# Scores of the next pair of heads, spread between the query tiles of the RWKV-7 stage

## The chip, the cores and the metric

The kernel runs on one core of one Trainium2 chip. The metric is the device time in microseconds of one execution of the whole program, as the median of the runs shown. Engines are named as the profile names them: PE is TensorE, DVE is VectorE, ACT is ScalarE, POOL is GpSimd, SP is SyncE, which issues most transfers.

## The reference, cut to what matters

The program is a two-layer diffusion backbone in float32 over 256 context and 256 latent tokens of width 1024. Layer 0 mixes tokens with a Hyena long convolution and a dense SwiGLU, layer 1 with bidirectional RWKV-7 and a top-2-of-8 expert SwiGLU. The change lies in RWKV-7, whose 16 heads of 64 channels follow this recurrence, forward and backward over context and latent tokens:

```
def step(S, inp):
    r_t, w_t, k_t, v_t, a_t, b_t = inp
    sa = jnp.einsum('bhvk,bhk->bhv', S, a_t)
    S = S * w_t[:, :, None, :] + sa[..., None] * b_t[:, :, None, :] + v_t[..., None] * k_t[:, :, None, :]
    return S, jnp.einsum('bhvk,bhk->bhv', S, r_t)
```

The kernel computes it in chunks of 64 tokens. Within a chunk it needs the products of all `a` with all `b` (called its own scores here), of `k` with `a` (key scores) and of `b` and `k` with the queries `r` (out scores), the inverse of a triangular matrix made from the own scores, and then one state per chunk boundary.

## The kernel before, in words

The heads are taken two at a time: eight pairs, `pair(i, more)`, each some 65 us long. Every engine has its own instruction stream, written out by hand, and each instruction waits on counting semaphores through `step(engine, group, name, pair)`: the names of a group stand in one ordered list (`_pair_steps`), and a wait is for a name's place in it. `settle` puts one wait-and-count instruction in the stream.

What a pair needs from the tokens themselves, called "ahead", is computed for the next pair while the present one runs: keys, rates, decays, values, queries and gate. TensorE's stream of a pair is, in order:

1. own scores S (line 1355, 32 products of 64x64 into banks 0 and 1; 64 matmul records, since each float32 product is two), key scores K (also line 1355, banks 2 and 3), out scores O (line 1375). S waits for VectorE's `a_1` of this pair and `g_ready_1` of the last, K for ScalarE's `out_copy`, O for ScalarE's `log_var`.
2. two turns of `At` (line 1223), which wait for ScalarE's copy of the gate out of bank 6.
3. the loop over four levels of the triangular inverse, 32x32 products: `level_first` (line 1299) waits for VectorE's transposed joins of S and, on entering the loop, for ScalarE's two score copies (line 2047), which themselves follow VectorE's joins of S (lines 2778 and 2781); then `level_second` (line 1310).
4. further turns, the last level, the keys of the next pair, products that build the chunk states (lines 1434 to 1504), and seven state steps (lines 1499 and 1504) with the tiles of the next pair's values (line 1273) between them. VectorE finishes `a_1` and `g_ready_1` before it makes the states of step 7.
5. the query tiles 0 to 3 of the next pair (line 1282, 128x256), the mean sum (line 1514), query tiles 4 to 7, the variance sum (line 1521), the gate products (lines 1289 and 1290). Then the next pair begins with S.

ScalarE at this place does, in order: `out_copy`, the square, the query copy (line 2027), Ln of the variance sum and Exp (lines 2095 and 2098, each with a table load), the gate copy (line 2031), the two score copies (line 2047). VectorE does `centred`, the multiplication of the queries with their decays, and then the joins of S, the masks of K and of O. SyncE loads the weights of the pair after next once the gate products are done (line 812). In the last pair the tiles of the output projection (line 1344, 128x256) stand between the state steps in place of the values.

Of the kernel before, what the change touches and what calls it, by code (L numbers as in the profile page):

```python
# [31 lines left out]
P = 128  # L32
D = 1024
KT = D // P
SEQ = 256
T = 2 * SEQ
NB = T // P
# [8 lines left out]
C = 64  # L46
# [123 lines left out]
def _pair_steps():  # L170


    pe = [f"{name}_{h}" for name in ("scored", "keys_scored", "out_scored") for h in range(2)]
    pe += ["a_turned_0", "a_turned_1", "b_turned_0", "b_turned_1", "k_turned_0", "k_turned_1", "v_turned"]
    pe += ["z_0", "z_1", "bonus_sum"]
    pe += [f"wu_{h}{d}" for h in range(2) for d in range(2)] + ["m_sum", "n_sum", "g_sum"]
    pe += [f"moved_{st}_{d}" for st in range(1, 7) for d in range(2)] + ["out_sum", "mean_sum", "var_sum"]

    act = ["score_copy_0", "score_copy_1", "a_copy_0", "a_copy_1", "b_copy_0", "b_copy_1", "k_copy_0", "k_copy_1"]
    act += ["v_copy", "spread_0", "spread_1", "z_copy_0", "z_copy_1"]  # L180
    act += [f"wu_copy_{h}{d}" for h in range(2) for d in range(2)]
    act += ["out_copy", "square", "log_var", "norm"]

    dve = []
    for h in range(2):
        dve += [f"joined_even_{h}", f"joined_0_{h}"]
    dve += ["keys_masked_0", "keys_masked_1", "out_masked_0", "out_masked_1", "chunk_decay"]
    dve += ["bonus", "inverse_0", "inverse_1", "n_ready_0", "n_ready_1", "state_1_0", "state_1_1"]
    dve += ["m_ready_0", "m_ready_1", "g_ready_0", "g_ready_1"]
    dve += [f"state_{st}_{d}" for st in range(2, 8) for d in range(2)]  # L190
    dve += ["centred"]
    finish = ["scaled", "shifted", "pair_out"]

    pool = ["g_start_0", "g_start_1", "gate_copy", "eye_0", "eye_1"]

    ahead_pe = ["keys", "rate_0", "rate_1", "decay_0", "decay_1", "key_sum", "values", "queries", "gate"]
    ahead_act = ["key_copy", "rate_sig_0", "rate_sig_1", "decay_sig_0", "decay_sig_1", "key_log", "key_norm"]
    ahead_act += ["e_incl_0", "e_inv_0", "e_excl_0", "e_incl_1", "e_inv_1", "e_excl_1"]
    ahead_act += ["value_copy", "query_copy", "gate"]
    ahead_dve = ["key_raw", "scan_0", "scan_1"]  # L200
    for d in range(2):
        ahead_dve += [f"rate_used_{d}", f"key_rated_{d}", f"bonus_key_{d}"]
    ahead_dve += ["key_unit"]
    for d in range(2):
        ahead_dve += [f"last_decay_{d}", f"k_{d}", f"b_{d}", f"a_{d}"]
    ahead_dve += ["r_0", "r_1", "bonus_query", "bonus_in"]
    ahead_pool = ["key_square", "b_raw_0", "b_raw_1", "next_digits"]
    return dict(pair_products=pe, pair_copies=act, pair_vectors=dve, pair_pool=pool, pair_finish=finish, ahead_products=ahead_pe,
                ahead_copies=ahead_act, ahead_vectors=ahead_dve, ahead_pool=ahead_pool)
# [44 lines left out]
def one(steps, name):  # L254


    names = STEPS[steps]
    assert names[PLACE[steps] % len(names)] == name, (steps, name, names[PLACE[steps] % len(names)])
    PLACE[steps] += 1
    return 1  # L260
# [74 lines left out]
def build(nc, a, out, consts):  # L335
    ctx = ExitStack()
    with ctx, nc.allow_non_contiguous_dma(reason="a few short columns"):
        sems = {}

        def sem(name):  # L340
            if name not in sems:
                sems[name] = ctx.enter_context(nc.semaphore(name))
            return sems[name]

        arena = ctx.enter_context(nc.sbuf_tensor("arena", [P, ARENA], F32))
        bank = [ctx.enter_context(nc.psum_tensor(f"bank{i}", [P, 512], F32)) for i in range(8)]
# [186 lines left out]
        last = mark()  # L533
# [122 lines left out]
        def hd(h):  # L656
            return slice(HN * h, HN * h + HN)

        def settle(eng):

            eng.sem_inc(sem("settled"), 1)
# [18 lines left out]
        def step(eng, steps, name, item):  # L680

            eng.wait_ge(sem(steps), (item + 1) * len(STEPS[steps]) + STEPS[steps].index(name) + 1)
# [188 lines left out]
        def _(pe):  # L871
# [405 lines left out]
            def ahead_queries(j, tiles):  # L1277
                if tiles[0] == 0:
                    pe.wait_ge(sem("ld_pair"), j * LD_PAIR + LD_QUERIES)
                    step(pe, "ahead_copies", "rate_sig_1", j)  # L1280
                for k in tiles:
                    last = mm(bank[7][:, 0:SEQ], wst[:, 0, k, :], XR[:, k, :], start=(k == 0), stop=(k == KT - 1))
                if tiles[-1] == KT - 1:
                    last.then_inc(sem("ahead_products"), one("ahead_products", "queries"))

            def ahead_gate(j):
                pe.wait_ge(sem("ld_pair"), j * LD_PAIR + LD_PAIR)
                step(pe, "ahead_copies", "value_copy", j)
                mm(bank[6][:, 0:SEQ], g2a, G1a, start=True, stop=False)
                mm(bank[6][:, 0:SEQ], g2b[0:32, :], G1b[0:32, :], start=False, stop=True)\  # L1290
                    .then_inc(sem("ahead_products"), one("ahead_products", "gate"))
# [46 lines left out]
            def out_products(first, last):  # L1338

                for t in range(first, last):  # L1340
                    k, m = t // KT, OUT_ORDER[t % KT]
                    if t % KT == 0:
                        pe.wait_ge(sem("ld_out"), 16 * (k + 1))
                    mm(out_sum(m), WO[k][:, m * P:(m + 1) * P], YT[:, k, :], start=(k == 0 and m % 2 == 0), stop=False,
                       skip_group_check=True)

            def pair(i, more):

                def scores(name, b0, left, right):
                    for x in range(2 * NB):  # L1350
                        d, b = divmod(x, NB)
                        for s_ in range(2):
                            t = slice(b * P + s_ * C, b * P + s_ * C + C)
                            for h in range(2):
                                last = mm(bank[b0 + h][hd(s_), x * C:x * C + C], left[d][hd(h), t], right[d][hd(h), t],
                                          start=True, stop=True)
                                if x == 2 * NB - 1 and s_ == 1:
                                    last.then_inc(sem("pair_products"), one("pair_products", f"{name}_{h}"))

                step(pe, "ahead_vectors", "a_1", i)  # L1360
                step(pe, "pair_vectors", "g_ready_1", i - 1)
                settle(pe)
                scores("scored", 0, At, Bt)
                step(pe, "pair_copies", "out_copy", i - 1)
                settle(pe)
                scores("keys_scored", 2, Kt, At)
                step(pe, "pair_copies", "log_var", i - 1)
                step(pe, "ahead_vectors", "r_1", i)
                settle(pe)
# [137 lines left out]
                last.then_inc(sem("pair_products"), one("pair_products", "out_sum"))  # L1507

                if more:
                    ahead_queries(i + 1, range(0, 4))  # L1510
                else:
                    out_products(16, 19)
                step(pe, "pair_copies", "out_copy", i)
                mm(bank[4][:, 0:SEQ], heads64, YF, start=True, stop=True)\
                    .then_inc(sem("pair_products"), one("pair_products", "mean_sum"))
                if more:
                    ahead_queries(i + 1, range(4, KT))
                else:
                    out_products(19, 23)
                step(pe, "pair_copies", "square", i)  # L1520
                mm(bank[5][:, 0:SEQ], heads64, YS, start=True, stop=True)\
                    .then_inc(sem("pair_products"), one("pair_products", "var_sum"))
                if more:
                    ahead_gate(i + 1)
                else:
                    out_products(23, OUT_TILES)

# [10 lines left out]
                ahead_values(0, [k])  # L1538
            pe.wait_ge(sem("xm_ready"), 6 * KT)
            ahead_queries(0, range(KT))  # L1540
            pe.wait_ge(sem("lora_taken"), 4)
            ahead_gate(0)
            for i in range(KT - 1):
                pair(i, True)
            pair(KT - 1, False)
# [791 lines left out]
        def _(dve):  # L2337
# [432 lines left out]
            def pair(i, more):  # L2770

                def first_join(h):
                    step(dve, "pair_products", f"scored_{h}", i)
                    step(dve, "pair_pool", f"eye_{h}", i - 1)
                    settle(dve)
                    scores = bank[h][:, :].rearrange("p (d b c) -> p d b c", d=2, c=C)
                    for j, name in enumerate(("joined_even", "joined_0")):
                        dve.copy_predicated(by_dir(TM[h], HC), each_block(first_bits[j]), scores[:, :, :, HC * j:HC * j + HC])\
                            .then_inc(sem("pair_vectors"), one("pair_vectors", f"{name}_{h}"))
                        step(dve, "pair_vectors", f"{name}_{h}", i)  # L2780
                    dve.transpose(TN[h].rearrange("p b c -> p (b c)"), TM[h].rearrange("p b c -> p (b c)"))\
                        .then_inc(sem("level_ready"), 1)
                    dve.sem_inc(sem("level_turned"), 1)
# [13 lines left out]
                for h in range(2):  # L2797
                    first_join(h)
                for h in range(2):
                    step(dve, "pair_products", f"keys_scored_{h}", i)  # L2800
                    dve.tensor_tensor(by_dir(AakT[h], C), by_dir(bank[2 + h][:, :], C), each_block(keys_mask), ALU.mult)\
                        .then_inc(sem("pair_vectors"), one("pair_vectors", f"keys_masked_{h}"))
                for h in range(2):
# [307 lines left out]
```

## Time and profile before

| | |
|---|---|
| median of 3 runs | 2436.03 us (2432.66 to 2442.88) |
| the profiled execution | 2433.53 us, its span 2431.7 us |
| mean granted TensorE clock | 0.982 |
| TensorE busy | 2327.2 us (96%) |
| VectorE, ScalarE busy | 1586.3 us (65%), 1265.7 us (52%) |
| chain that ended last | PE 91%, DVE 3%, issue 3%, ACT 1%, DMA 1% |
| the eight pairs of heads | some 840 to 1362 us of the span |

The chain that ended last is followed back from the last instruction; "issue" in it, and as a releaser of idle time, is time in which an engine waited for nothing that the profile shows. A matmul record overlaps its neighbours, so the distance from start to start tells what it takes in a stream, and its own duration does not.

### The profile page before, as it was taken

How to read it: one execution, taken by the hardware profiler on the slowest of the kernel's cores; microseconds unless marked ns; L12 is line 12 of the kernel's file. 1: busy time of each engine (PE TensorE's matmuls, PEld its weight loads, DVE VectorE, ACT ScalarE, POOL GpSimd, SP SyncE). 2: the span in 40 equal slices, each digit the busy share in tenths (PEclk: the TensorE clock that was granted, in tenths of full speed). 3: DMA queues.
4: the chain of work that ended last, by engine and by line, in shares of the span. 5: the costliest groups of instructions: out<-in, count | busy, mean ns of one | idle time of the engine just before them, and what ended most of it. 6: DMA issues, size and time to landing. Idle time of an engine off the chain costs nothing.

```text
span 2431.7 us, 57067 instructions
## 1 busy us (share of the span) xinstructions
PE 2327.2 (96%) x24762; PEld 1889.2 (78%) x24762; DVE 1586.3 (65%) x1810; ACT 1265.7 (52%) x1400; POOL 208.8 (9%) x196
## 2 busy tenths in 40 slices
PE   8999999999999888988988899999999999999998
PEld 5677576888887466767766688988888888888887
DVE  3544876222333945555555388888888888888887
ACT  4322025222222844444434277777777777777774
POOL 2000642000000221111111000000000000000000
PEclk9999999999999999999989999999999999999999
DMA  8465126333224201111112469999999999999993
GB/s 295 171 242 219 52 87 173 87 103 87 100 91 133 89 23 32 32 32 32 32 32 72 175 257 365 338 368 335 368 333 369 333 370 337 366 338 363 342 362 133
DMA packets 249079, 490.41 MB, mean 202 GB/s; under 512 B 14615, under 2 KB 107567, under 8 KB 248623
## 3 DMA queue, kind: packets, MB, share of 16 engines
q1 hardware_dynamic: 247214, 481.31, 55.8%
q10 hardware_dynamic: 1730, 7.10, 0.9%
q8 instruction: 109, 1.79, 0.3%
q14 instruction: 26, 0.21, 0.0%
HBM read 486.29 MB, written 2.10 MB: 201 GB/s over the span
## 4 chain that ended last, share of the span: by engine, by line
PE 91%; DVE 3%; issue 3%; ACT 1%; DMA 1%; SPq 0%; POOL 0%; DVEq 0%; ACTq 0%
PE bank L1626 26%; PE bank L1653 13%; PE bank L1159 3%; PE bank L1160 3%; PE bank L1161 3%; PE bank L1299 2%; PE bank L1273 2%; PE bank L1065 2%; PE bank L1036 2%; PE bank L1310 2%; PE bank L1037 2%; PE bank L1038 2%; PE bank L1177 2%; PE bank L1176 2%; PE bank L1178 2%
## 5 line engine op out<-in xcount | busy, mean ns | idle before, releaser
L2970 DVE TENSOR_TENSOR w_low<-expert_w,w_high 128x1792 fp32r<-128x1792 f32 (+2 forms) x384 | 769.1, 2024 | 125.3 <-ACT w_high L2169 123.6
L2169 ACT CAST w_high<-expert_w 128x1792 fp32r<-128x1792 f32 (+2 forms) x384 | 652.9, 1701 | 247.0 <-PE bank L1626 154.3
L1626 PE MATMUL bank<-w_high,xg_high 128*128 128x448 f32 x1024 | 294.5, 369 | 4.0 <-DVE xg_low L2960 4.0
L1626 PE MATMUL bank<-w_low,xg_high 128*128 128x448 f32 x1024 | 292.1, 367 | 0.0
L1626 PE MATMUL bank<-w_high,xg_low 128*128 128x448 f32 x1024 | 291.7, 366 | 0.0
L1626 PEld LDWEIGHTS bank<-w_high,xg_high 128*128 128x128 f32 x1024 | 191.5, 189 | 19.9 <-DVE xg_low L2960 4.2
L1626 PEld LDWEIGHTS bank<-w_low,xg_high 128*128 128x128 f32 x1024 | 193.4, 189 | 15.3
L1626 PEld LDWEIGHTS bank<-w_high,xg_low 128*128 128x128 f32 x1024 | 193.2, 189 | 15.2
L1653 PE MATMUL bank<-w_high,hid_high 128*128 128x512 f32 x448 | 175.4, 392 | 0.0
L1653 PE MATMUL bank<-w_high,hid_low 128*128 128x512 f32 x448 | 174.7, 390 | 0.0
L1653 PE MATMUL bank<-w_low,hid_high 128*128 128x512 f32 x448 | 174.5, 389 | 0.0
L1159 PE MATMUL bank<-u_high,ring_high 128*128 128x512 f32 x352 | 139.4, 396 | 2.1 <-DVE u_low L2615 2.0
L1160 PE MATMUL bank<-u_low,ring_high 128*128 128x512 f32 x352 | 139.1, 395 | 0.0
L1161 PE MATMUL bank<-u_high,ring_low 128*128 128x512 f32 x352 | 138.5, 393 | 0.0
L2634 DVE TENSOR_TENSOR arena<-arena,bank 128x512 f32 (+1 forms) x22 | 15.1, 688 | 127.5 <-ACT arena L1932 127.5
L1653 PEld LDWEIGHTS bank<-w_high,hid_low 128*128 128x128 f32 x448 | 84.1, 188 | 17.8
L1653 PEld LDWEIGHTS bank<-w_low,hid_high 128*128 128x128 f32 x448 | 84.2, 188 | 16.7
L1653 PEld LDWEIGHTS bank<-w_high,hid_high 128*128 128x128 f32 x448 | 84.2, 188 | 16.6
L1932 ACT ACTIVATE arena<-bank 128x512 f32<-128x512 f32 x22 | 13.2, 599 | 158.9 <-PE bank L1161 158.9
L2788 DVE COPY_PREDICATED arena<-arena,bank 128x256 f32<-128x256 int32 x64 | 28.4, 444 | 81.7 <-PE bank L1310 81.7
L1159 PEld LDWEIGHTS bank<-u_high,ring_high 128*128 128x128 f32 x352 | 66.6, 189 | 18.1 <-issue 2.9
L2037 ACT COPY arena<-bank 128x256 f32<-128x256 f32 x80 | 29.4, 382 | 97.5 <-PE bank L1299 97.4
(427 smaller groups left out, 4106.8 us busy)
## 6 DMA issues: line engine op xcount, KB each, us to landing
expert_w<-in_moe_w_dram SPq DMA_DIRECT2D x192, 1792.0 KB, 9.4
arena<-in_mod_w_dram SPq DMA_DIRECT2D x48, 1024.0 KB, 8.1
arena<-in_ffn_w_dram SPq DMA_DIRECT2D x44, 512.0 KB, 5.1
arena<-in_hy_w_in_dram SPq DMA_DIRECT2D x12, 1024.0 KB, 5.2
arena<-in_rw_w_rkv_dram SPq DMA_DIRECT2D x48, 256.0 KB, 2.7
arena<-in_ffn_w_dram SPq DMA_DIRECT2D x11, 1024.0 KB, 4.8
arena<-in_hy_w_out_dram SPq DMA_DIRECT2D x4, 1024.0 KB, 9.1
arena<-in_rw_w_out_dram SPq DMA_DIRECT2D x8, 512.0 KB, 3.5
```

Of the source, the lines that this page charges most:

```text
L1036: pe.matmul(bank[m % 4][:, :], wh[:, k, :], uh, start=(k == 0), stop=False)
L1037: pe.matmul(bank[m % 4][:, :], wh[:, k, :], ul, start=False, stop=False)
L1038: last = pe.matmul(bank[m % 4][:, :], wl[:, k, :], uh, start=False, stop=(k == KT - 1))
L1065: last = pe.matmul(bank[2 * part + f][:, :], fwd[:, tt, (2 * part + f) * P:(2 * part + f + 1) * P], ZT[:, 2 * s + tt, half * 512:half * 51 ...
L1159: pe.matmul(bank[b + h][:, :], wh[:, c, :], uh, start=(k == 0), stop=False)
L1160: pe.matmul(bank[b + h][:, :], wh[:, c, :], ul, start=False, stop=False)
L1161: last = pe.matmul(bank[b + h][:, :], wl[:, c, :], uh, start=False, stop=(k == KT - 1))
L1176: pe.matmul(bank[m][:, :], wh[:, o, :], hh, start=first, stop=False)
L1626: last = pe.matmul(bank[b0 + v][:, 0:EH], x[:, k, :], w_[:, kk, v * EH:v * EH + EH], start=(k == 0 and x is XGH and w_ is wh), stop=(k == ...
L1653: last = pe.matmul(bank[4 + half][:, :], x[:, f, :], w_[:, f - 4 * i_, :], start=(c == 0 and f == 0 and x is HTH and w_ is wh), stop=(c == ...
L2169: act.copy(high_piece(kind, n), piece(kind, ering[q % ERN], n // 2, n % 2))\
L2970: dve.tensor_tensor(piece(kind, low[s], n // 2, n % 2), piece(kind, ering[s], n // 2, n % 2), high_piece(kind, n).bitcast(F32), ALU.subtract)\
```

## The change

Line 1355's products leave `pair` and become two functions of a range of blocks. The own scores of the next pair are issued block by block, each block (4 products, 8 records) behind the query tile of the same number. The key scores of the next pair are issued in two halves, the first four blocks between the variance sum and the gate products, the other four behind the gate. Their semaphore names move from the group `pair_products` to `ahead_products`, and VectorE waits for them there. The waits that S and K had stand before their first blocks as before. In front of the first pair all own scores stand between queries and gate, and all key scores behind the gate. The number of products, waits and copies is the same.

```
-    pe = [f"{name}_{h}" for name in ("scored", "keys_scored", "out_scored") for h in range(2)]
+    pe = [f"{name}_{h}" for name in ("out_scored",) for h in range(2)]
...
+    ahead_pe = ["keys", "rate_0", "rate_1", "decay_0", "decay_1", "key_sum", "values", "queries", "scored_0", "scored_1",
+                "gate", "keys_scored_0", "keys_scored_1"]
...
+            def scores(i, name, b0, left, right, blocks):
+                if blocks[0] == 0:
+                    if name == "scored":
+                        step(pe, "ahead_vectors", "a_1", i)
+                        step(pe, "pair_vectors", "g_ready_1", i - 1)
+                    else:
+                        step(pe, "pair_copies", "out_copy", i - 1)
+                    settle(pe)
+                for x in blocks:
+                    d, b = divmod(x, NB)
+                    for s_ in range(2):
+                        t = slice(b * P + s_ * C, b * P + s_ * C + C)
+                        for h in range(2):
+                            last = mm(bank[b0 + h][hd(s_), x * C:x * C + C], left[d][hd(h), t], right[d][hd(h), t],
+                                      start=True, stop=True)
+                            if x == 2 * NB - 1 and s_ == 1:
+                                last.then_inc(sem("ahead_products"), one("ahead_products", f"{name}_{h}"))
...
                 if more:
-                    ahead_queries(i + 1, range(0, 4))
+                    for k in range(4):
+                        ahead_queries(i + 1, range(k, k + 1))
+                        own_scores(i + 1, range(k, k + 1))
...
                 if more:
-                    ahead_queries(i + 1, range(4, KT))
+                    for k in range(4, KT):
+                        ahead_queries(i + 1, range(k, k + 1))
+                        own_scores(i + 1, range(k, k + 1))
...
                 if more:
+                    key_scores(i + 1, range(4))
                     ahead_gate(i + 1)
+                    key_scores(i + 1, range(4, 2 * NB))
...
             ahead_queries(0, range(KT))
+            own_scores(0, range(2 * NB))
             pe.wait_ge(sem("lora_taken"), 4)
             ahead_gate(0)
+            key_scores(0, range(2 * NB))
```

## Rows read from the trace of the kernel before

**Rows 1.** The page, busy time and share of the span, instructions.

```profile
PE 2327.2 (96%) x24762; PEld 1889.2 (78%) x24762; DVE 1586.3 (65%) x1810; ACT 1265.7 (52%) x1400; POOL 208.8 (9%) x196
```

**Rows 2.** Waits of PE, 905 to 1316 us: line, releaser, us, times, longest.

```profile
PE bank L1310 <- issue: 17.2, 7, 3.0
PE bank L1299 <- issue: 5.6, 11, 1.5
```

**Rows 3.** DMA queues, 905 to 1316 us: packets, MB, share of 16 engines.

```profile
q8 instruction: 61, 1.00, 1.0%
```

**Rows 4.** Timeline of PE, pair 2 to 3: start us, us, instruction, count, idle before.

```profile
972.97 1.99 PE L1282 MATMUL bank<-arena 128*128 128x256 f32 x8
975.23 1.89 PE L1282 MATMUL bank<-arena 128*128 128x256 f32 x8
977.39 0.59 PE L1289 MATMUL bank<-arena 128*128 128x256 f32 x2
978.54 2.10 PE L1355 MATMUL bank<-arena 64*64 64x64 f32 x128
980.45 1.11 PE L1375 MATMUL bank<-arena 64*64 64x64 f32 x64
983.18 1.58 PE L1299 MATMUL bank<-arena 32*32 32x32 f32 x128 [0.60 <-DVE arena L2781]
984.65 0.39 PE L1310 MATMUL bank<-arena 32*32 32x32 f32 x22
...
987.48 0.75 PE L1310 MATMUL bank<-arena 32*32 32x32 f32 x49 [2.45 <-issue]
```

**Rows 5.** Timeline of ACT at the same place.

```profile
977.16 0.38 ACT L2027 COPY arena<-bank 128x256 f32<-128x256 f32 x1 [0.85 <-PE bank L1282]
977.55 1.28 ACT L2095 ACT_TABLE_LOAD   x1
...
980.96 0.35 ACT L2031 COPY arena<-bank 128x256 f32<-128x256 f32 x1
...
982.15 0.59 ACT L2047 COPY arena<-bank 128x512 f32<-128x512 f32 x1 [0.35 <-DVE arena L2778]
```

**Rows 6.** Timeline of PE, state steps of the last pair.

```profile
1353.21 0.33 PE L1499 MATMUL bank<-arena 64*64 64x64 f32 x4
...
1353.82 1.13 PE L1344 MATMUL bank<-arena 128*128 128x256 f32 x4
1354.88 0.33 PE L1499 MATMUL bank<-arena 64*64 64x64 f32 x4
```

**Rows 7.** Timeline of PE, pair 3 to 4.

```profile
1045.20 0.45 PE L1375 MATMUL bank<-arena 64*64 64x64 f32 x13 [1.71 <-issue]
1045.58 1.09 PE L1223 MATMUL bank<-arena 128*128 128x128 f32 x8
...
1049.36 0.39 PE L1299 MATMUL bank<-arena 32*32 32x32 f32 x24 [1.46 <-issue]
1049.57 1.25 PE L1310 MATMUL bank<-arena 32*32 32x32 f32 x103
1053.77 0.43 PE L1310 MATMUL bank<-arena 32*32 32x32 f32 x16 [2.95 <-issue]
```

**Rows 8.** Timeline of PE, first level of pairs 2, 5, 6, 7 and 8.

```profile
919.80 0.92 PE L1310 MATMUL bank<-arena 32*32 32x32 f32 x68
923.09 1.07 PE L1310 MATMUL bank<-arena 32*32 32x32 f32 x60 [2.37 <-issue]
...
1114.28 0.97 PE L1299 MATMUL bank<-arena 32*32 32x32 f32 x70 [0.98 <-issue]
...
1118.14 1.09 PE L1310 MATMUL bank<-arena 32*32 32x32 f32 x62 [2.37 <-issue]
...
1181.02 1.16 PE L1310 MATMUL bank<-arena 32*32 32x32 f32 x108 [2.11 <-issue]
...
1247.82 0.74 PE L1310 MATMUL bank<-arena 32*32 32x32 f32 x37 [2.31 <-issue]
...
1312.84 0.87 PE L1310 MATMUL bank<-arena 32*32 32x32 f32 x49 [2.68 <-issue]
```

More of the change, by code:

```diff
@@ L194, in _pair_steps @@
     pool = ["g_start_0", "g_start_1", "gate_copy", "eye_0", "eye_1"]
-    ahead_pe = ["keys", "rate_0", "rate_1", "decay_0", "decay_1", "key_sum", "values", "queries", "gate"]
+    ahead_pe = ["keys", "rate_0", "rate_1", "decay_0", "decay_1", "key_sum", "values", "queries", "scored_0", "scored_1",
+                "gate", "keys_scored_0", "keys_scored_1"]
     ahead_act = ["key_copy", "rate_sig_0", "rate_sig_1", "decay_sig_0", "decay_sig_1", "key_log", "key_norm"]
@@ L1345, in out_products, with own_scores, key_scores @@
                        skip_group_check=True)
-            def pair(i, more):
[L1349 to L1366, printed above, removed]
+            def scores(i, name, b0, left, right, blocks):
[15 more added lines that the diff above has]
+                                last.then_inc(sem("ahead_products"), one("ahead_products", f"{name}_{h}"))
+            def own_scores(i, blocks):
+                scores(i, "scored", 0, At, Bt, blocks)
+            def key_scores(i, blocks):
+                scores(i, "keys_scored", 2, Kt, At, blocks)
+            def pair(i, more):
                 step(pe, "pair_copies", "log_var", i - 1)
@@ L2772, in first_join @@
                 def first_join(h):
-                    step(dve, "pair_products", f"scored_{h}", i)
+                    step(dve, "ahead_products", f"scored_{h}", i)
                     step(dve, "pair_pool", f"eye_{h}", i - 1)
@@ L2799, in pair @@
                 for h in range(2):
-                    step(dve, "pair_products", f"keys_scored_{h}", i)
+                    step(dve, "ahead_products", f"keys_scored_{h}", i)
                     dve.tensor_tensor(by_dir(AakT[h], C), by_dir(bank[2 + h][:, :], C), each_block(keys_mask), ALU.mult)\
```

## The prediction

> **What bounds the kernel now.** I read the page first, then the waits of TensorE over the seven hand-overs between pairs of heads, then the timeline of one hand-over. TensorE is busy 96% of the span [rows 1]. Over the pair stage its idle time is not put down to another engine but to "issue": 17.2 us at the second half of the first level (L1310) and 5.6 us at its first half (L1299) [rows 2]. The timeline of pair 3 shows the form: L1310 runs 22 matmuls and stops, and goes on at 987.48, though nothing it waits for is open [rows 4]. Pair 4 stops three times, going on at 1045.20, 1049.36 and 1053.77. Between the first two stand 13 + 8 + 104 matmuls (the last count is 128 minus the 24 of the next row), between the last two 24 + 103 [rows 7]: 125 and 127 matmuls, with as many weight loads and a few waits 256 instructions each time. The instruction queue of the DMA moved 61 packets of 16.4 KB [rows 3]. So code arrives in blocks of 256 instructions, and where TensorE runs small matmuls (128 records of L1355 start within 1.9 us [rows 4]) it outruns the loading. One block costs 4.16 and 4.41 us there, 3.86 in pair 5 [rows 8]; in pair 7, whose rows repeat the pattern of pair 4, 4.2 to 4.6. The counts place the boundaries of the other pairs. Pair 2 stops 68 matmuls into L1310; 128 matmuls before that is 68 into L1299, which it passes at 919.2 without a stop, and 128 before that, the turns and waits taken off, is some 15 into O, passed at 915.65. So a block is there 3.55 us after the crossing before it where TensorE ran on (pair 8: 3.6). I take 3.6 from such a crossing and 3.9 from a stop.
>
> The scores (S: 32 products, 64 records; K: the same) stand in a stretch that has both things: full TensorE, and code that is too late. The change trades one against the other.
>
> **The change, part by part.** No product, wait or copy is added or taken away, and the code in front of each pair's out scores (L1375, called O) has the same length. So from O on the block boundaries lie where they lie now. All times below are in the frame of pair 3, whose S starts at 978.54; the other six hand-overs have the same rows 65.02 us earlier (pair 2) and 62.06, 129.41, 194.04, 255.80 and 324.82 us later.
>
> *1. S moves between the tiles of the queries.* A tile is two records of 128x256 in 0.43 us; a block of S is 8 records of 64x64. The products themselves stream at 0.117 us a block (1.91 us for 16 blocks [rows 4]). What it costs to go from the full array to 64x64 and back, the last pair shows: there two tiles of 128x256 alternate with 16 small records. From 1353.21 to 1354.88 is 1.67 us [rows 6]; the four large records take 0.86, the small ones, in eight steps of 0.0585, 0.47. What is left is 0.34 us per round trip, and the rows name no idle time in front of the small group or the large one. The same subtraction with the values' 128x512 records gives 0.35 in the other pairs. At eight blocks, seven of which stand ahead of the last query tile: 7 x (0.117 + 0.347) = 3.25 us later for the end of the queries. Bounds: 0 and 0.347 for the trip, so 0.8 to 3.3 us; I take the upper one, since the row has this very shape.
>
> The Trainium skill says under "TensorEngine Tiling (Array Packing)", Key Properties, that a change of tiling mode drains the engine. By that rule the price is real; it names no figure.
>
> *2. K stands around the gate.* One more trip (K, gate, K) and the one behind the variance sum: 0.7 us of TensorE. It lies beside ScalarE, as the next step shows, and costs nothing; without that cover it would be 0.7 us a pair.
>
> *3. What sets the start of the levels.* Now: the query copy follows the last query tile at once (977.16); behind it, in order, come two table loads with Ln and Exp, the gate copy (980.96 to 981.31) and the two score copies [rows 5]. The second one starts at 982.15, held 0.35 us by VectorE's joins, and L1299 starts 0.44 us after its end (982.74 to 983.18 [rows 4, 5]). After: the joins find S done early, so the copies follow the gate copy at once: 981.31 + 2 x 0.59 = 982.49, a gain of 0.25 us. TensorE has done its part by then: variance sum, four blocks of K, gate (1.25 us), four blocks of K, O and the turns end 0.2 us before the copies. So S leaves a place where ScalarE's chain covers nearly all of it: of 0.95 us moved only 0.25 is won, and what is late next is that chain. The chain starts with the last query tile, which is 3.25 later: the levels start 3.0 us later, at 986.18.
>
> *4. The code.* What this makes of the hand-over depends on where the boundary lies. Call B the one at O and C the next, in L1299; D is the one in L1310, where all pairs stop. The variance sum, now 0.43 before the gate products at 977.39, moves by all eight blocks, 8 x 0.464, to 980.7; it takes 0.6, four blocks of K 0.65, the gate 1.25, four blocks 0.5, a trip at each change of size among them [rows 4], so O starts at 983.7 (980.45 now).
> Pairs 3 and 6: B lies in K, C just behind the start of the levels, so C and D move with them: +2.9 each (now D is at 987.48 and, for pair 6, at 1181.02 [rows 4, 8]).
> Pair 2: B at 983.9, code of C there at 987.5, D 3.9 later at 991.4; now 923.09 + 65.02 = 988.1 [rows 8]: +3.3.
> Pair 8: B 983.6, C 987.2, D 991.1; now 1312.84 - 324.82 = 988.0: +3.1.
> Pair 5: B 983.8, C 987.35, D 991.25; now 1118.14 - 129.41 = 988.7: +2.5.
> Pairs 4 and 7: these stop at B and C too. B is now 50 and 39 matmuls into O, and its block is asked for only inside S; in the new order that point falls ahead of the variance sum, over 6 us before it is needed. The stops at O (1.7 and 2.0 us) go, those in L1299 shrink to some 0.4. B 984.4, C 988.0, D 992.0, against 1053.77 - 62.06 = 991.7 [rows 7] and 1247.82 - 255.80 = 992.0 [rows 8]: +0.5 (its blocks are slow) and -0.2.
> The first pair stays: its S waits for VectorE's a_1 in either order, and its three late blocks follow from that: 0, bounds -1 and +1.
>
> From D on nothing is changed; the rest of each pair follows with the same waits. Sum: 2.9 + 2.9 + 3.3 + 3.1 + 2.5 + 0.5 - 0.2 = **+15.0 us**. On the profiled execution's 2433.5 us (span 2431.7) that is 2448.5. The median shown is 2.5 us higher, 2436.0, and gives 2451; I say 2450, +0.6%.
>
> *Small things.* The loads of the next pair's weights are released by the gate, now some 4 us later; its first tile is used over 20 us after, so they cost nothing, and their packets meet the same code blocks as today. VectorE's masks of K come later against the levels' start by less than the join that follows needs. Both 0, bounds 0 and +0.5 a pair.
>
> **Rivals.**
> *The trip costs and the code gives nothing back.* If the block time grows with the load beside it, so that pairs 4, 5 and 7 keep their three stops, each hand-over pays 3.0: +21, 2457. For it: the blocks of pair 7 took 4.5 and 4.2 us, not 3.8. Against: their stops end at fixed instructions, and TensorE gets more time ahead of them.
>
> *The trip costs nothing between queries, and the time is not longer.* In the row that I priced it by, a wait instruction stands ahead of each small group; between S blocks there is none behind the first. If the weights of the next group are then loaded beside the running tile, the queries end 0.82 later, the levels start 0.57 later, pairs 4 and 7 win 2.5 each, pair 5 0.4 and the other four lose 0.57: -3.1, 2433. It decides once a trip is below 0.1 us, since five hand-overs then lose less than 1.2. For it: between products of one size the weight loads do run ahead. Against: the query row behind the small products of L1504, where nothing is waited for either, takes 1.99 us, and the one behind a product of its own size 1.89, for the same eight records [rows 4]; that is the weight load of the first one laid bare, 0.1 us by itself.
> The Trainium skill, "TensorE: Matmul & The Clock Gate", Step-by-step, lets TensorE's window pull weight loads ahead of running matmuls where row groups don't conflict; that is this rival. [...]
>
> *The code wins more.* As the last, and in pairs 2, 5 and 8 C and D come early too, with the stops before D gone (1.7 + 1.5, 0.3 + 1.0, 2.0 + 1.4 = 7.9 us), and S's 0.95 us saved whole: -14, 2422. Against: the chain of copies starts no earlier, so D cannot.
>
> *It doesn't do what it says:* S could be held at its first block by a_1 or g_ready_1. Both are done before state 7, which TensorE has passed: no time, within the forecast.
>
> **How the numbers follow.** Forecast 0.60, of it 0.43 above the line; the second case, all trips and no relief, 0.16; the free trip 0.16; the code wins more 0.08. Within 0.5% (12.2 us) this kernel's measurement tells nothing from no change: up to 2448.2. The forecast's own spread is some 5 us around +15, as blocks take 3.6 to 4.5 us and the runs shown lie within 10. Slower: 0.43 + 0.15 = 0.58. Faster by over 0.5%, below 2423.9, takes the last case nearly whole: 0.07. The rest is 0.35. The range leaves out 0.1 on either side: 2433, which holds the free trip's centre, to 2459, above the case without relief.
>
> **What would show it.** In the profile after: query records L1282's line in pairs with 8 small records between, about 0.9 us from block to block; if it is 0.55, step 1 fails. The start of L1299 3.0 us later after the first query tile (now 983.18 - 972.97 = 10.2, then 13.2 [rows 4]). No stop in O in pairs 4 and 7. TensorE's busy time up, its "issue" idle down by some 6 us. The prediction is wrong if hand-overs 3 and 6 don't lose about 3 us, or if pairs 4 and 7 do.

## The result and the profile after

The changed kernel takes 2450.36 us (median of 4 runs, 2443.89 to 2453.91) against 2437.36 us (2432.66 to 2442.88): a ratio of 1.0068, 95% interval 1.005 to 1.0087. It is slower by 13 us, where 2450 was forecast. A second comparison (the run `c_after` below) gave 1.0077, 1.0063 to 1.0091, which is some 19 us; its medians, 2454.07 and 2433.14, are 21 us apart. The profiled execution is the quickest of the four, 2443.89 us with a span of 2442.1.

First the page: busy time and share of the span, and the waits of TensorE over the seven hand-overs, 905 to 1330 us (L1311 and L1300 are L1310 and L1299 of before, [rows 1, 2]).

```profile
PE 2342.2 (96%) x24762; PEld 1881.5 (77%) x24762; DVE 1585.9 (65%) x1810; ACT 1264.6 (52%) x1400; POOL 209.2 (9%) x196
```

```profile
PE bank L1311 <- issue: 18.9, 7, 3.5
PE bank L1300 <- issue: 6.8, 18, 1.3
```

TensorE has the same 24762 records and is busy 15 us longer. A busy engine that does the same work in more time is one whose records are spaced wider. Where, the timeline of the hand-over to pair 3 shows, in the order of [rows 4] (L1283 is the query tile, L1361 the scores, L1532 the variance sum):

```profile
975.94 0.70 PE L1283 MATMUL bank<-arena 128*128 128x256 f32 x2
976.57 0.34 PE L1361 MATMUL bank<-arena 64*64 64x64 f32 x8
976.84 0.70 PE L1283 MATMUL bank<-arena 128*128 128x256 f32 x2
...
983.60 0.70 PE L1532 MATMUL bank<-arena 128*128 128x256 f32 x2
984.23 0.69 PE L1361 MATMUL bank<-arena 64*64 64x64 f32 x32
984.86 0.70 PE L1290 MATMUL bank<-arena 128*128 128x256 f32 x2
985.48 0.69 PE L1291 MATMUL bank<-arena 32*128 32x256 f32 x2
986.11 0.69 PE L1361 MATMUL bank<-arena 64*64 64x64 f32 x32
986.62 1.11 PE L1382 MATMUL bank<-arena 64*64 64x64 f32 x64
987.67 1.09 PE L1224 MATMUL bank<-arena 128*128 128x128 f32 x8
989.00 1.56 PE L1300 MATMUL bank<-arena 32*32 32x32 f32 x128 [0.24 <-issue]
...
993.08 1.17 PE L1311 MATMUL bank<-arena 32*32 32x32 f32 x106 [2.28 <-issue]
```

A query tile and a block of own scores come every 0.90 us (975.94 to 976.84). Their own streaming is 0.43 + 0.117; the other 0.35 is one trip between the sizes (from the full array to 64x64 products and back). No idle column names it. From the first query tile to the levels (the first product of L1300) it is 989.00 - 975.94 = 13.06 us. Before it was 10.21. ScalarE's part, for [rows 5]:

```profile
983.43 0.37 ACT L2042 COPY arena<-bank 128x256 f32<-128x256 f32 x1 [2.27 <-PE bank L1283]
983.82 1.28 ACT L2110 ACT_TABLE_LOAD   x1
...
987.23 0.35 ACT L2046 COPY arena<-bank 128x256 f32<-128x256 f32 x1
987.48 1.08 ACT L2062 COPY arena<-bank 128x512 f32<-128x512 f32 x2
```

The two score copies are one row now: the second no longer waits for VectorE's joins. The rows from the query copy to the end of the copies follow each other with no idle time.

Pair 8 (first block of rows) gives the clearest view of the stops for code, pair 4 (second block) of what is won back [rows 7, 8]:

```profile
1320.98 0.59 PE L1300 MATMUL bank<-arena 32*32 32x32 f32 x47 [0.24 <-issue]
1322.84 1.03 PE L1300 MATMUL bank<-arena 32*32 32x32 f32 x81 [1.27 <-issue]
1323.72 0.58 PE L1311 MATMUL bank<-arena 32*32 32x32 f32 x45
1327.81 1.38 PE L1311 MATMUL bank<-arena 32*32 32x32 f32 x83 [3.51 <-issue]
```

```profile
1051.35 1.11 PE L1382 MATMUL bank<-arena 64*64 64x64 f32 x64
1052.39 1.09 PE L1224 MATMUL bank<-arena 128*128 128x128 f32 x8
1053.73 1.24 PE L1300 MATMUL bank<-arena 32*32 32x32 f32 x104 [0.24 <-issue]
1055.31 0.39 PE L1300 MATMUL bank<-arena 32*32 32x32 f32 x24 [0.34 <-issue]
1055.52 1.25 PE L1311 MATMUL bank<-arena 32*32 32x32 f32 x103
1059.17 0.57 PE L1311 MATMUL bank<-arena 32*32 32x32 f32 x25 [2.40 <-issue]
```

The stops stand behind the same counts of matmuls as before (103 and 104 in pair 4, 45 in pair 8): the boundaries didn't move against the levels. In pair 4 the stop at O is gone, and that in L1300 is down from 1.46 to 0.34. Here and below C is the boundary that falls into L1300 and D the one in L1311, as in the forecast.

From the first query tile to the end of the last stop (D), in us:

| pair | 2 | 3 | 4 | 5 | 6 | 7 | 8 | sum |
|---|---|---|---|---|---|---|---|---|
| before | 15.1 | 14.5 | 18.7 | 15.7 | 14.0 | 19.0 | 15.1 | 112.2 |
| after | 19.1 | 17.1 | 18.5 | 19.4 | 17.4 | 18.4 | 19.9 | 129.8 |
| difference | +3.9 | +2.6 | -0.2 | +3.6 | +3.4 | -0.6 | +4.8 | +17.6 |
| forecast | +3.3 | +2.9 | +0.5 | +2.5 | +2.9 | -0.2 | +3.1 | +15.0 |

This sum repeats: 130.2 in the second execution of the same kernel. What lies behind the last D does not: 1118.9 us before, 1114.3 after, 1121.9 in that second execution. It is one reason why the profiled spans differ by 10.4, the medians by 13 and those of the second comparison by 21. So the experiments are read by the hand-overs first, and by the time of the whole second.

### The profile page after: what moved, and what is told of

The parts are those of the page before. It is cut to its first block, busy times and chain, and to the rows that moved or that the text cites. A ratio compares the mean times of both kernels' runs of the same rounds, so it can differ in the third digit from the quotient of the medians.

```text
span 2442.1 us, 57067 instructions
## 1 busy us (share of the span) xinstructions
PE 2342.2 (96%) x24762; PEld 1881.5 (77%) x24762; DVE 1585.9 (65%) x1810; ACT 1264.6 (52%) x1400; POOL 209.2 (9%) x196
## 4 chain that ended last, share of the span: by engine, by line
PE 92%; DVE 3%; issue 3%; ACT 1%; DMA 1%; SPq 0%; POOL 0%; ACTq 0%; DVEq 0%
PE bank L1641 26%; PE bank L1668 13%; PE bank L1160 3%; PE bank L1161 3%; PE bank L1162 3%; PE bank L1300 2%; PE bank L1274 2%; PE bank L1066 2%; PE bank L1037 2%; PE bank L1038 2%; PE bank L1039 2%; PE bank L1311 2%; PE bank L1178 2%; PE bank L1177 2%; PE bank L1179 2%
## 5 line engine op out<-in xcount | busy, mean ns | idle before, releaser
L2649 DVE TENSOR_TENSOR arena<-arena,bank 128x512 f32 (+1 forms) x22 | 15.1, 688 | 127.5 <-ACT arena L1947 127.5
L1160 PEld LDWEIGHTS bank<-u_high,ring_high 128*128 128x128 f32 x352 | 66.6, 189 | 18.2 <-issue 2.9
```

The costliest lines, as they stand in the source:

```text
L1160: pe.matmul(bank[b + h][:, :], wh[:, c, :], uh, start=(k == 0), stop=False)
```

## The experiments

Theory A is the forecast's: trips between sizes delay the last query tile, ScalarE's chain hands that on, and code in blocks of 256 instructions decides how much of it reaches D. Each rival is in the expectations.

**c_after.** The changed kernel, unedited.

> The changed kernel again, on the chip of the next three. Theory A (each trip from the full array to 64x64 products and back costs 0.35 us; seven of them delay the last query tile, and ScalarE's chain passes that on to the levels): from the first query tile to the first product of the levels 13.1 us in pairs 2 to 8 (before: 10.2, in pairs 4 and 7 11.6 and 11.9); whole kernel +0.5 to +0.7% against before. Theory B (the loss is chance of the run, or of the split keys): the distance varies between executions by more than 1 us.

Measured: 2454.07 us, ratio 1.0077 (1.0063 to 1.0091). Tile to levels 13.06 or 13.07 in six pairs and 13.31 in pair 5; D sum 130.2. The distance is a property of the order, not of the run. A single pair's D moves by up to 0.28 us between these two executions of one kernel; smaller differences of a pair are not read.

**e1_two_tiles.** Fewer trips, the same products in the same stretch.

```
-                    for k in range(4):
-                        ahead_queries(i + 1, range(k, k + 1))
-                        own_scores(i + 1, range(k, k + 1))
+                    for k in range(0, 4, 2):
+                        ahead_queries(i + 1, range(k, k + 2))
+                        own_scores(i + 1, range(k, k + 2))
...
```

> Two query tiles, then two blocks of own scores: three trips ahead of the last two query tiles where the change has seven. Theory A: the last tile ends 6 x 0.117 + 3 x 0.347 = 1.7 us late and not 3.25, the levels start 11.6 us after the first query tile, and the kernel takes some 9 us less than the change (about +6 against before). Theory B (trips are free, the loss is in the products moved or in the split keys): 13.1 us still, no difference to the change.

Measured: 2443.37 us, ratio 1.0028 (1.0014 to 1.0041), against c_after's 1.0077 on the same chip: 11 us less. Tile to levels 11.53 to 11.62 (11.95 in pair 5), D sum 118.5, so +6.3 against before. The cycle in pair 3, two tiles and two blocks:

```profile
980.90 1.13 PE L1283 MATMUL bank<-arena 128*128 128x256 f32 x4
981.96 0.46 PE L1361 MATMUL bank<-arena 64*64 64x64 f32 x16
982.35 1.13 PE L1283 MATMUL bank<-arena 128*128 128x256 f32 x4
```

From start to start (982.35 - 980.90) it is 1.45 us; less 0.86 for the tiles and 0.23 for the blocks that leaves 0.35 again, for twice the products. The price is by trip, not by product, and theory A's number holds.

**e2_whole.** No trip ahead of the last query tile.

```
-                    for k in range(4, KT):
-                        ahead_queries(i + 1, range(k, k + 1))
-                        own_scores(i + 1, range(k, k + 1))
+                    ahead_queries(i + 1, range(4, KT))
+                    own_scores(i + 1, range(2 * NB))
...
-                    key_scores(i + 1, range(4))
                     ahead_gate(i + 1)
-                    key_scores(i + 1, range(4, 2 * NB))
+                    key_scores(i + 1, range(2 * NB))
```

(The first four tiles stand in one call again, too.)

> Own scores in one group between the last query tile and the variance sum, key scores in one group behind the gate. Theory A: the last query tile is not delayed at all; variance sum 1.3 us later, covered by ScalarE's table load; the levels start 10.0 us after the first query tile, 0.25 earlier than before, because the score copies no longer wait for the joins; the stops for code at O in pairs 4 and 7 go (2.5 us each). Sum about -7 us against before. Theory B (own scores ahead of the gate cost by being there): levels at 11 us or later, slower than before.

Measured: 2430.82 us, ratio 0.9994 (0.9983 to 1.0006): no difference to before. The mechanism came as expected, tile to levels 9.91 (10.29 in pair 4), and no pair stops at O. The sum did not: D at 110.7 in all, 1.5 below before where 7 was expected. Pair 3:

```profile
981.02 1.09 PE L1224 MATMUL bank<-arena 128*128 128x128 f32 x8
982.04 1.72 PE L1300 MATMUL bank<-arena 32*32 32x32 f32 x128
983.64 0.38 PE L1311 MATMUL bank<-arena 32*32 32x32 f32 x22
987.02 1.18 PE L1311 MATMUL bank<-arena 32*32 32x32 f32 x72 [3.00 <-issue]
```

The levels start 0.3 us earlier, and the stop in L1311 is 3.0 us where it was 2.45 [rows 4]: here the earlier start is waited away at D. It is not so in every pair. Pairs 4 and 7, which no longer stop at O, end 1.5 and 3.5 us earlier (17.3 and 15.6), pair 5 stays, and the other four end 0.4 to 1.3 us later, 3.4 together; pair 6 stops in L1300, where it did not before. So the relief came, 4.9 us of the 5 expected, and what was missed is that D comes later in the others.

**e3_keys_whole.** The change, with the keys unsplit: the last hunk of e2 alone.

> The change with the key scores back in one group behind the gate. Theory A: the split costs TensorE 0.35 us, but beside ScalarE's chain: levels still at 13.1 us, total within 1 us of the change. Theory B (the split keys carry the loss): levels at 12 us or earlier, 5 to 10 us faster than the change.

Measured: 2445.32 us, ratio 1.0054 (1.0037 to 1.0071), c_after 1.0077 beside it. TensorE reaches O 0.36 us earlier (10.33 after the first tile, 10.69 in the change), and the levels start at 13.06, as in the change: one trip less on TensorE and nothing gained there. D sum 127.4, 2.4 to 2.8 less. Of that the levels' start explains nothing; the D distances move by -1.0, +0.7, -0.4, -1.2, +0.4, +0.7 and -1.5, both ways, as code blocks do. The total missed the 1 us expected. It is 0.23% below c_after (5.6 us, with intervals that meet), and by the medians 8.8 us, which is the size that theory B gave. The levels' start speaks against B's way to it. What the split keys cost the whole kernel, beyond nothing at the levels, stays open.

**e8_no_tables.** e3 with the table loads taken out of the chain.

```
-                act.activation(YS, bank[5][:, 0:SEQ], ACT.Ln, bias=eps[:, 1:2])\
+                act.copy(YS, bank[5][:, 0:SEQ])\
...
-                act.activation(YS, YS, ACT.Exp, scale=-0.5).then_inc(sem("pair_copies"), one("pair_copies", "norm"))
+                act.activation(YS, YS, ACT.Copy, scale=0.5).then_inc(sem("pair_copies"), one("pair_copies", "norm"))
```

> The change with the key scores whole behind the gate, and Ln and Exp of the output's variance replaced by plain copies, so that ScalarE needs no table load between the last query tile and the score copies (the logarithm and the exponential of that norm are left out). Theory A (ScalarE's chain holds the levels): 2.5 us go from the chain, TensorE's own order becomes the bound, and the levels start 12.4 to 12.7 us after the first query tile, where it was 13.06. Theory B (TensorE's queue or VectorE's joins hold them): 13.0 still.

Measured: tile to levels 12.40 in six pairs, 12.64 in pair 5. (Its total, 3442.68 us, is not read: other values go into the router, and the experts' loop makes a second pass.) With e3 this shows the chain: TensorE faster by 0.36 moves nothing, ScalarE freed moves the levels by 0.66. D sum 125.0 beside e3's 127.4, so of 7 x 0.66 = 4.6 us only 2.4 reach D; the rest goes into code stops.

**e4_same_size.** Own scores ahead of all query tiles, next to products of their own size.

```
                 if more:
-                    for k in range(4):
-                        ahead_queries(i + 1, range(k, k + 1))
-                        own_scores(i + 1, range(k, k + 1))
+                    own_scores(i + 1, range(2 * NB))
+                    ahead_queries(i + 1, range(0, 4))
...
```

> Own scores in one group directly behind the last state product, which is 64x64 too, so ahead of all query tiles and with no trip added; key scores in one group behind the gate. In the first pair the queries then wait behind the own scores for VectorE's a_1, about +5 us once. Theory A (trips): the queries start 0.94 us later and nothing else delays them; from the first query tile to the levels 9.9 us; pairs 2 to 8 together within 3 us of before, kernel +3 to +8 with the first pair. Theory B (own scores early cost by being early): the distance plus the 0.94 is above 12 us, kernel as slow as the change.

Measured: 2450.04 us, ratio 1.0063 (1.0048 to 1.0078), and the expected +3 to +8 was wrong. In pairs 3, 4, 6 and 8 the distance from tile to levels is 9.76 to 9.86, as theory A says. In pairs 2 and 5 it is 11.45, in pair 7 13.42. Pair 2:

```profile
910.80 0.88 PE L1361 MATMUL bank<-arena 64*64 64x64 f32 x42
914.12 0.57 PE L1361 MATMUL bank<-arena 64*64 64x64 f32 x22 [2.44 <-issue]
914.62 3.56 PE L1283 MATMUL bank<-arena 128*128 128x256 f32 x8
```

The state steps and the own scores together are small products without a gap, and a boundary falls among the scores: 2.44 us of stop. Behind it eight query records take 3.56 us, not 1.99: the granted clock of the stretch is 0.54, which is the 1.2 GHz level (the columns are the stretch, its length, the busy times and counts of PE, PEld, DVE, ACT and POOL, the clock, the DMA share and GB/s).

```profile
914.60:918.00 3.40, 3.40 (x15) 2.68 (x10) 0.00 (x0) 0.00 (x0) 0.00 (x0) 0.54 0.00 0
```

Pair 5 stops for 2.16 us at the same place, and pair 7 for 1.70 us in the query tiles. So theory A's trips were rightly priced, and what I left out was that the place had no slack in code. The scores' own 0.94 us a pair is not won back either: from the first tile, without them, D comes only 0.5 to 1.5 us earlier in pairs 3, 4, 6 and 8, and 0.7 to 1.7 later in pairs 2, 5 and 7. The first pair adds some 3.5 us, where 5 were expected: the end of its last stop in L1311 is 863.08, and was 859.56 in L1310.

**e5_shift.** The kernel before, its code moved by half a block.

```
                 settle(pe)
+                if i == 0:
+                    for n in range(32):
+                        mm(bank[4 + n % 2][hd(n // 2 % 2), 0:C], At[0][hd(n % 2), 0:C], Bt[0][hd(n % 2), 0:C], start=True, stop=True)
                 scores("scored", 0, At, Bt)
```

> The kernel before with 32 extra 64x64 products (128 instructions, half a block of code, about 0.5 us, their results overwritten) once, in the first pair behind the wait of its own scores. Theory A (code comes in blocks of 256 instructions): all boundaries move 64 matmul records ahead against the products. From the first query tile to the end of the stop in L1310, or in L1299 where it moves there: pair 3 from 14.5 to about 19, pair 8 from 15.1 to about 19, pair 4 from 18.7 to about 15, pair 7 from 19.0 to about 14.5, pair 2 from 15.1 to 14; stops at O vanish from pairs 4 and 7 and appear in 3 and 8. Total near +3 us. Theory B (the stops belong to these lines or to a wait): every pair keeps its own distance within 0.5 us, +0.5 us in all.

Measured, tile to D: pair 2 14.3, pair 3 18.8, pair 4 14.4, pair 5 19.3, pair 6 16.2, pair 7 14.0, pair 8 18.9. Each of the five numbers given came within 0.6 us. Pair 3, which stopped once, now stops three times, at the counts that 64 records less give (33 in O, 86 in L1299, 85 in L1310; it was 22 in L1310):

```profile
977.15 0.69 PE L1378 MATMUL bank<-arena 64*64 64x64 f32 x33
979.01 0.69 PE L1378 MATMUL bank<-arena 64*64 64x64 f32 x31 [1.18 <-issue]
979.64 1.09 PE L1223 MATMUL bank<-arena 128*128 128x128 f32 x8
980.66 1.12 PE L1299 MATMUL bank<-arena 32*32 32x32 f32 x86
983.95 0.56 PE L1299 MATMUL bank<-arena 32*32 32x32 f32 x42 [2.17 <-issue]
984.37 1.39 PE L1310 MATMUL bank<-arena 32*32 32x32 f32 x85
988.42 0.85 PE L1310 MATMUL bank<-arena 32*32 32x32 f32 x43 [2.67 <-issue]
```

The stops belong to places in the code, not to lines or waits. The total missed: 2430.53 us, ratio 0.9988 (0.9978 to 0.9997), a little faster where +3 was expected; the hand-overs are 3.5 us longer, and the rest of the profiled execution is shorter (1112.9 us behind D). The shift also moves the code of everything later, the experts' loops too. Whether that or the spread of the executions made up for it stays open. It also says how little 0.1% of the whole shows: hand-overs that are 3.5 us longer measured faster.

**e6_late_loads.** The change, its weight loads later.

```
                 step(sp, "ahead_products", "gate", i - 1)
+                if i:
+                    sp.wait_ge(sem("level_products"), level_product(i - 1, 1, 0, 0))
                 cols = slice(i * P, i * P + P)
```

> The change, with the loads of the next weights held back until the second level of the next pair's inverse has begun, so that no weight load lies beside the code blocks C and D. Theory A (the extra 3.4 us in pairs 2, 5 and 8 are code blocks slowed by the loads beside them): D 0.5 to 1.5 us earlier in pairs 2, 5 and 8, 0 to 0.5 in the others, 3 to 6 us less than the change in all. Theory B (a block takes its time with or without loads): no pair moves by more than 0.5 us and the total stays.

Measured: 2448.76 us, ratio 1.0058 (1.0044 to 1.0072). Tile to D: 17.7, 17.1, 18.2, 18.5, 17.2, 18.4, 19.3, sum 126.5, 3.3 less than the change; pairs 2, 5 and 8 gain 1.4, 0.8 and 0.6, the others 0 to 0.3. The total is no witness: its interval overlaps those of both comparisons of the change. Pairs 2 and 5 are what theory A expected. Pair 8 is the control, since its loads are those of the kept residual, which this edit leaves where they are. The rows are the 3 us that begin 15 us after the first query tile; the last number is GB/s. First the change in pairs 4, 5 and 8, then this run in pairs 5 and 8:

```profile
1055.66:1058.66 3.00, 1.11 (x108) 0.96 (x95) 0.44 (x1) 0.37 (x1) 0.00 (x0) 1.00 0.18 51
1122.08:1125.08 3.00, 1.44 (x127) 1.27 (x126) 0.00 (x0) 0.74 (x2) 0.00 (x0) 0.81 0.32 93
1322.91:1325.91 3.00, 1.39 (x126) 1.27 (x127) 0.00 (x0) 0.74 (x2) 0.00 (x0) 0.90 0.33 92
```

```profile
1123.22:1126.22 3.00, 1.16 (x121) 1.05 (x118) 0.00 (x0) 0.71 (x2) 0.00 (x0) 0.84 0.02 5
1323.56:1326.56 3.00, 1.09 (x109) 1.00 (x109) 0.00 (x0) 0.75 (x2) 0.00 (x0) 1.00 0.30 87
```

From the end of the stop at C to the end of that at D the change takes 3.87 us in pair 4 and 3.67 in pair 7, but 4.39, 4.41 and 4.96 in pairs 2, 5 and 8, the three with 88 to 93 GB/s there. Without the loads pair 5 takes 3.87; pair 8, which keeps them, still 4.69. So loads beside a block go with a slower block, and in pair 5 taking them away gave half a us (in c_after, the change once more, it takes 4.42).

**e7_whole_late.** e2 and e6 together.

> Own scores whole behind the last query tile, key scores whole behind the gate, and the late loads. Theory A: 3 to 6 us below the same order with early loads, so some 6 us below before (-0.25%). Theory B: as that order, -0.1%.

Measured: 2429.34 us, ratio 0.9977 (0.9964 to 0.999), D sum 107.4, 4.8 below before and 3.3 below e2. It beats the kernel before by 0.23%, within 0.1 to 0.36%, and the change by some 0.9%. That is near theory A's -0.25%, with B's -0.1% at the edge of the interval. How much of it the late loads bring shows only in the D sum, since the intervals of e2 and e7 overlap.

## Why the prediction was right

*Trips (step 1).* Forecast 0.347 each, from the state steps of the last pair. Measured 0.35 in the change and 0.35 in e1. The rival in which they are free between queries is out: the cycle is 0.90 us and not 0.55.

*The split keys (step 2).* At the levels' start they cost nothing (e3: 13.06 with and without). At D they may: 2.4 us in all, within what code blocks move both ways. The whole kernel measured 5.6 us faster without the split, with intervals that meet, so the forecast's 0 is shown for the levels alone.

*The chain (step 3).* Levels 3.0 us later was forecast, 2.85 measured (13.06 against 10.21). Its two parts: the query copy comes 7.49 us after the first tile and not 4.19, so 3.30 later (forecast 3.25); from its start to the end of the score copies it is 5.13 us (983.43 to 988.56) and not 5.58, so 0.45 won (forecast 0.25). e3 and e8 show that ScalarE holds the levels: in e3's order TensorE could have begun them 0.66 us earlier, so in the change's own, where it comes 0.36 later, some 0.3.

*The code (step 4).* The shape came: pairs 4 and 7 lose nothing (-0.2 and -0.6 against +0.5 and -0.2), the stop at O goes, D moves with the levels in 3 and 6. e5 shows the blocks themselves. The sizes were off where the new order lets a block come late: pair 2 +3.9 for 3.3, pair 5 +3.6 for 2.5, pair 8 +4.8 for 3.1. These three were reckoned with 3.9 us from C to D and took 4.39, 4.41 and 4.96. The 3.6 us for a block after a crossing without a stop was a bound read as a size: at 919.2 the code was there, and the row doesn't say since when.

One sign of the forecast failed. TensorE's idle time put down to "issue" was to fall by some 6 us. Over O and the two halves of the first level (905 to 1330 us) it went from 26.9 us to 25.7. The 4.0 us at O went, as forecast, but the two halves of the level rose from 22.9 to 25.7: 2.8 of the 4.0 us won at O came back at C and D.

*The small things.* This is the term that should not have been nothing. I had put the loads released by the gate at 0, with packets that "meet the same code blocks as today". They don't: the loads start 2.7 us before the levels in the new order (986.29 in the second row below), 4.5 before them in the old (978.71 in the first row, against 983.18), and lie over another block.

```profile
978.71 2.99 SPq L812 DMA_DIRECT2D arena<-in_rw_w_rkv_dram  x2
```

```profile
986.29 2.93 SPq L813 DMA_DIRECT2D arena<-in_rw_w_rkv_dram  x2
991.35 0.34 SPq L819 DMA_DIRECT2D arena<-in_rw_w_dram  x1
```

With them held back (e6) the hand-overs are 3.3 us shorter, 2.2 of it in pairs 2 and 5 and 0.6 in pair 8, whose loads did not move; the sum is then +14.3, beside a forecast of 15.0. Pair 8 stays 1.2 us over its forecast: its loads are still there, but no run took them away, so that part is not shown.

*The sum.* +15.0 forecast, +17.6 in the hand-overs, +13 between the medians, +10.4 between the profiled spans. The difference of the spans is 17.6 less 0.8 ahead of the first query tile of all (839.14 for 839.92), 0.7 in the first pair, 1.2 between the hand-overs and 4.6 behind them. That last part is not the change's: it varies by 9 us over ten executions of nine kernels, and by 7.6 between the two of the change. So the closeness of 2450 to 2450.4 is in part luck; a forecast of 17.6 would have said 2453, and the second comparison measured 19 to 21 where 15 was forecast.

The rival "the code gives nothing back" (+21, pairs 4, 5 and 7 keeping three stops) is out by the table. "The code wins more" is out too: it needed D to come early in pairs 2, 5 and 8, and there D came later or stayed, in e2 (+0.6, 0.0 and +1.1) as in the change.

## What to carry to other kernels

Filling TensorE with small products between large ones costs by the number of changes of size, and the price is invisible as idle time: look for the same work with more busy time, and keep products of one size together. Before moving work to fill an engine, ask which instruction of the engine behind it the new place delays: here the last query tile starts ScalarE's chain. And where unrolled code of small instructions stops without a releaser, count instructions between the stops. If the count is constant, much of an earlier start is only waited for at the next one, and what lies beside the loading of the code counts too (3.3 us for the loads in e6). The place of the code moves single stages by up to 5 us (e5); no run here shows a place that makes the sum shorter.

## What the runs showed that was not expected

- The same code shifted by 128 instructions moved single stages by 4 to 5 us either way (pair 3 from 14.5 to 18.8, pair 7 from 19.0 to 14.0), so a comparison of two orders in one stage can be one of alignments.
- A 2.44 us stop of TensorE was followed by a stretch at a granted clock of 0.54, so that it cost some 4 us in all (eight records took 3.56 us instead of 1.99).
- Taking 0.66 us out of the way to the levels in each of seven hand-overs gave 2.4 us at their ends, not 4.6.
- The stop for a block of code was longer where 88 to 93 GB/s of loads ran ahead of it (4.4 to 5.0 us from block to block, for 3.7 to 3.9).
